# An encoder step with an expert layer: block loops written out, the end of a block taken apart

## The reference, cut to what matters

```python
def block(xb):                                   # PEER, xb: 128 normed tokens
    qh = (xb @ wq).reshape(PEER_BLOCK, PEER_HEADS, 2, PEER_HALF)
    s1 = jnp.einsum('thd,nd->thn', qh[:, :, 0], keys1)
    s2 = jnp.einsum('thd,nd->thn', qh[:, :, 1], keys2)
    v1, i1 = lax.top_k(s1, PEER_TOPK)
    v2, i2 = lax.top_k(s2, PEER_TOPK)
    ...                                          # 16 x 16 sums, top 16 of them: sc, e
    gate = jax.nn.softmax(sc, axis=-1)
    act = jax.nn.gelu(jnp.einsum('td,thkd->thk', xb, u_tab[e])) * gate
    return jnp.einsum('thk,thkd->td', act, v_tab[e])
...
hp = hp + yp                                     # yp: the mixer
hp = hp + peer(rmsnorm(hp, norm_ffn[l]), *pw)
...
y_prompt = rmsnorm(hp[:, N_META:], norm_final)
```

## Time and profile before

| what | value |
|---|---|
| median of 3 runs | 3307.91 us (3298.36 to 3314.12) |
| the profiled execution's own time | 3304.53 us |
| its span, first to last instruction | 3302.3 us |
| TensorE matmul busy | 2607.0 us (79%) |
| VectorE busy | 2282.9 us (69%) |
| GpSimd busy | 2004.0 us (61%) |
| ScalarE busy | 648.6 us (20%) |
| mean granted TensorE clock | 0.852 |
| DMA moved | 1213.81 MB, mean 368 GB/s |

### The profile page before, as it was taken

One profiled execution on the slowest core, in us unless ns is written; L12 is line 12 of the kernel. 1 busy time (PEld: TensorE's weight loads), 2 busy tenths in 40 slices (PEclk: granted clock), 3 DMA queues, 4 the chain that ended last, 5 costly groups with the idle time before them and its releaser, 6 DMA issues.

```text
span 3302.3 us, 42154 instructions
## 1 busy us (share of the span) xinstructions
PE 2607.0 (79%) x11764; PEld 1183.6 (36%) x11764; DVE 2282.9 (69%) x6088; ACT 648.6 (20%) x2367; POOL 2004.0 (61%) x2131
## 2 busy tenths in 40 slices
PE   7687888778887788778887788778887788777666
PEld 2563453234422453234422453234422453233111
DVE  2454987678756887679756887578766887679453
ACT  2221222111211222111211122112211222111111
POOL 0132567665776567665766567665776567665775
PEclk9798999878997889878987899878997889888557
DMA  7354999999999999999999999999999999999998
GB/s 263 135 197 166 387 363 394 416 390 344 396 405 403 377 368 395 409 391 349 399 402 398 376 368 398 407 392 343 404 413 400 371 368 399 403 398 359 398 399 362
DMA packets 340171, 1213.81 MB, mean 368 GB/s; under 512 B 41072, under 2 KB 41200, under 8 KB 339904
## 3 DMA queue, kind: packets, MB, share of 16 engines
q0 software_dynamic: 304128, 1107.43, 85.8%
q1 hardware_dynamic: 35776, 103.32, 8.3%
HBM read 1205.73 MB, written 4.87 MB: 367 GB/s over the span
## 4 chain that ended last, share of the span: by engine, by line
PE 25%; DMA 25%; DVE 24%; issue 15%; POOL 6%; ACT 3%; POOLq 0%; DVEq 0%; ACTq 0%; SPq 0%
DMA ring<-peer_v,idxv 16%; PE bank L458 15%; PE acc L458 10%; DMA ring<-peer_u,idx 9%; DVE ring L1434 8%; POOL ring L434 6%; DVE kw L1211 2%; DVE eh L1222 1%; DVE kw L1221 1%; DVE topi L1213 1%; DVE kw L1219 1%; ACT xn L857 1%; DVE idxv L1269 1%; DVE tops L1212 1%; DVE topi L1214 1%
## 5 line engine op out<-in xcount | busy, mean ns | idle before, releaser
L458 PE MATMUL acc<-ring,wv 128*32 128x512 f32 x4224 | 1312.9, 709 | 540.4 <-DMA ring<-peer_v,idxv 417.7
L1434 DVE SCALAR_TENSOR_TENSOR ring<-ring,xcur 128x1024 f32<-128x1024 f32 x1056 | 1283.6, 1218 | 656.4 <-DMA ring<-peer_u,idx 630.6
L434 POOL DMA_INDIRECT ring<-peer_u,idx x1056 | 1006.6, 953 | 817.7 <-issue 416.3
L434 POOL DMA_INDIRECT ring<-peer_v,idxv x1024 | 964.0, 941 | 433.5 <-issue 277.1
L458 PEld LDWEIGHTS acc<-ring,wv 128*32 128x32 f32 x4224 | 171.3, 115 | 1203.2 <-issue 662.7
L458 PEld LDWEIGHTS bank<-xT,win 128*128 128x128 f32 (+1 forms) x2304 | 276.2, 190 | 108.5 <-issue 92.9
L458 PE MATMUL bank<-xT,win 128*128 128x128 f32 (+1 forms) x2304 | 307.1, 290 | 6.8 <-DVE kw L1232 4.3
L857 ACT ACTIVATE wv<-rep,coefv 128x32 f32<-128x32 f32 x1024 | 264.3, 312 | 109.4 <-PE acc L458 79.4
L458 PEld LDWEIGHTS bank<-xT,qk 128*128 128x128 f32 x1024 | 160.1, 246 | 64.5 <-issue 64.5
L458 PE MATMUL bank<-win,xT 128*128 128x512 f32 (+3 forms) x368 | 177.3, 614 | 1.9 <-ACT xT L857 1.9
L458 PE MATMUL bank<-xT,qk 128*128 128x128 f32 x1024 | 173.1, 338 | 0.0
(11 more groups left out here) (232 smaller groups left out, 2213.8 us busy)
## 6 DMA issues: line engine op xcount, KB each, us to landing
qk<-wq SPq DMA_DIRECT2D x64, 512.0 KB
t<-wq SPq DMA_DIRECT2D x64, 512.0 KB, 6.9
ring<-peer_u,idx POOLq DMA_INDIRECT x1056, 6.5
ring<-peer_v,idxv POOLq DMA_INDIRECT x1024, 6.6
win<-w_in SPq DMA_DIRECT2D x6, 2048.0 KB, 15.3
ring<-wq SPq DMA_DIRECT2D x16, 512.0 KB, 5.2
wout<-w_out SPq DMA_DIRECT2D x1, 4096.0 KB, 22.4
xn<-x_prompt SPq DMA_DIRECT2D x8, 512.0 KB, 6.9
```

Source lines behind the costliest of these rows:

```text
L434: pool.indirect_dma_start(out=ring[:, slot, :], out_offset=None, in_=(peer_u, peer_v)[which], in_offset=bass.IndirectOffsetOnAxis(ap=rows_ ...
L458: return nc.tensor.matmul(out, lhsT, rhs, start=start, stop=stop)
L1434: stt(row, row, 1.0, xcur[:, :], ALU.mult, ALU.mult, accum_out=dots[:, column(b, e):column(b, e) + 1]).then_inc(s_dot, 1)
```

## The change

The five loops over blocks become Python loops, so that the code of every block stands in the program. What `is_count` and `looped` ask of a block's number is answered for each. At a block's end:

- TensorE's `take_up` is left to the sample alone. The first four V sums of a block open the banks of `acc` themselves (`start=opens`), the first of them after a wait for `s_acc_out`. The residual is added in ticks 22 to 25 by the new `add_residual`, one group of 32 tokens a tick, two matmuls of the shape of a V sum.
- ScalarE's `finish` is parted: `take_sums` (the copies out of `acc`) runs in tick 18 of the next block after that tick's `weights`, and raises `s_acc_out` at its end. `square_sums` runs in tick 19: squares of two halves into `xc`, an addition, Ln and Exp.
- VectorE's `finish` (the last norm, and with it `s_y`) runs at the beginning of tick 21.
- VectorE's waits in `query` for `s_acc0` and for V sums of the block before are taken out.
- SyncE's order stays as it is.

```diff
@@ constants
+T_RESIDUAL = LAG + GROUPS
@@ looped
-            return not isinstance(v, int)
+            return v > 2
@@ SyncE, GpSimd, TensorE, ScalarE, VectorE: the same edit in each
-            with sp.Fori(0, BLOCKS - 1) as b:
+            for b in range(BLOCKS - 1):
                 load_wq(b, range(10, 12))
                 load_x(b + 1, x_prompt[bass.ds(b * P + P, P), :])
                 load_wq(b, range(12, 16))
...
@@ TensorE: take_up keeps the sample's part alone
-                if b is None:
-                    pe.wait_ge(s_topk, 2)
-                else:
-                    pe.wait_ge(s_acc_out, streams_before(b))
-                if b is None:
-                    for half in range(2):
-                        last = mm(acc[0:n, 512 * half:512 * half + 512], ident[0:n, 0:n], h[0:n, 512 * half:512 * half + 512], stop=False)
-                else:
-                    mm(acc[:, 0:512], ident[:, :], h[:, 0:512], stop=False)
-                    for to, of in ((0, 64), (64, 0)):
-                        last = mm(acc[to:to + 64, 512:1024], ident[:, of:of + 64], h[:, 512:1024], stop=False)
+                pe.wait_ge(s_topk, 2)
+                for half in range(2):
+                    last = mm(acc[0:n, 512 * half:512 * half + 512], ident[0:n, 0:n], h[0:n, 512 * half:512 * half + 512], stop=False)
                 last.then_inc(s_acc0, 1)
+
+            def add_residual(b, tick):
+
+                g = tick - T_RESIDUAL
+                if not 0 <= g < GROUPS:
+                    return
+                if g == 0:
+                    pe.wait_ge(s_h2, streams_before(b) + 1)
+                for half in range(2):
+                    lo = SAMPLE * ((g + GROUPS // 2 * half) % GROUPS)
+                    last = mm(acc[lo:lo + SAMPLE, 512 * half:512 * half + 512], ident[:, SAMPLE * g:SAMPLE * g + SAMPLE],
+                              h[:, 512 * half:512 * half + 512], start=False, stop=False)
+                if g == GROUPS - 1:
+                    last.then_inc(s_acc0, 1)
@@ TensorE: expert_sum
+                opens = b is not None and j < GROUPS
+                if b is not None and j == 0:
+                    pe.wait_ge(s_acc_out, streams_before(b))
...
-                              ring[:, slot, 512 * half:512 * half + 512], start=False, stop=final)
+                              ring[:, slot, 512 * half:512 * half + 512], start=opens, stop=final)
@@ TensorE: the blocks
-            take_up(0)
-            with pe.Fori(0, BLOCKS - 1) as b:
+            for b in range(BLOCKS - 1):
                 for tick in range(LAG, BLOCK_TICKS):
                     expert_sum(b, tick - LAG)
+                    add_residual(b, tick)
                     beside(b, tick, True)
...
-                take_up(b + 1)
@@ ScalarE: finish is parted
-            def finish(b):
+            def take_sums(b):
...
-                    link(a(y, acc[0:n, :], ACT.Copy))
+                    last = a(y, acc[0:n, :], ACT.Copy)
                 else:
                     a(y[:, 0:512], acc[:, 0:512], ACT.Copy)
                     for to, of in ((0, 64), (64, 0)):
                         last = a(y[to:to + 64, 512:1024], acc[of:of + 64, 512:1024], ACT.Copy)
-                    link(last)
-                link(a(acc[0:n, :], y, ACT.Square, accum_out=stat[0:n, 6:7]))
-                act.sem_inc(s_acc_out, 1)
+                last.then_inc(s_acc_out, 1)
+
+            def square_sums(b):
+
+                n = n_experts(b)
+                y = xn[0:n, :]
+                junk = xc[:, :, :].rearrange("p f t -> p (f t)")[0:n, :]
+                act.wait_ge(s_acc_out, streams_before(b) + 1)
+                link(a(junk, y[:, 0:512], ACT.Square, accum_out=stat[0:n, 8:9]))
+                link(a(junk, y[:, 512:1024], ACT.Square, accum_out=stat[0:n, 7:8]))
+                link(a(stat[0:n, 6:7], stat[0:n, 7:8], ACT.Identity, bias=stat[0:n, 8:9]))
                 rstd(n, 6, D_MODEL).then_inc(s_rstd_y, 1)
+
+            def finish(b, tick):
+
+                done = b - 1 if b else None
+                if tick == LAG:
+                    restart()
+                    take_sums(done)
+                if tick == LAG + 1:
+                    square_sums(done)
@@ ScalarE: the blocks (after the last block take_sums and square_sums follow each other)
-            finish(None)
...
                     weights(b, tick - LAG)
+                    finish(b, tick)
                     beside(b, tick, True)
@@ VectorE: query
-                    if tick >= LAG and head > 0:
-                        dve.wait_ge(s_acc0, streams_before(b) + 1)
-                    elif not is_count(b, 0):
-                        dve.wait_ge(s_vsum, experts_before(b - 1) + TOPK * head + TOPK)
+                    if head >= PEER_HEADS - SAMPLE // TOPK:
+                        dve.wait_ge(s_vsum, SAMPLE)
@@ VectorE: the blocks
-            finish(None)
-            with dve.Fori(0, BLOCKS - 1) as b:
+            for b in range(BLOCKS - 1):
                 restart()
                 for tick in range(LAG, BLOCK_TICKS):
+                    if tick == LAG + 3:
+                        finish(b - 1 if b else None)
...
-                finish(b)

```

More of the change, by code:

```diff
@@ L448, in _ @@
             gathers(first + over(0), None)
-            with pool.Fori(0, BLOCKS - 1) as b:
+            for b in range(BLOCKS - 1):
                 gathers(side_by_side(b, range(LAG, P)) + over(b + 1), over(b)[-RING:])
@@ L1126, in _ @@
                 beside(0, tick, False)
-            finish(None)
-            with act.Fori(0, BLOCKS - 1) as b:
-                restart()
+            for b in range(BLOCKS - 1):
                 for tick in range(LAG, BLOCK_TICKS):
@@ L1158, in _ @@
                     spread_coef(b, PEER_HEADS - 1, tick)
-            finish(b)
+            take_sums(b)
+            square_sums(b)
         @block.vector
@@ L1530, in _ @@
             for tick in range(LAG, BLOCK_TICKS):
+                if tick == LAG + 3:
+                    finish(b - 1)
                 if tick % TOPK == 0:
```

## The result

The changed kernel takes 3346.78 us (median of 4 runs, 3340.25 to 3350.46); the kernel before, beside it on the same chip, 3311.01 us. The ratio is 1.0113, 95% interval 1.008 to 1.0146: slower. The profiled execution of the changed kernel took 3345.1 us against 3304.5 before, 40.6 us more, where the prediction's sum had 26.0. In the code after, the dot is L1458, `gmax` L1264, `tops` L1236, `idxv` L1293, the norm L1489; TensorE's helper is L459, SyncE's tile load L323, its store L336.

What follows compares the result with a forecast made beforehand. VectorE's path across each block's end was taken as the bound. Ends -43.6, norm +10.3, tile wait +46.1, spread +12.2, rest +1.0 sum to +26.0 us on the profiled 3304.53 us; forecast 3333 us, range 3290 to 3358.

Steps and rivals of the forecast that it cites:

- The gain at the ends: VectorE, last choice of a block to the next dot: the gap shrinks to 0.1 us, 43.6 us gained in all.
- The norm: VectorE, tick 21: the moved norm still costs 1.29 us an end, 10.3 us for eight.
- ticks 18 to 20 keep their shape: Ticks after the end: 9.3 us from the first dot to that of tick 21, as before.
- SyncE's queue: Tiles 10 and 11 stand behind the store awaiting the later norm; VectorE waits 5.8 us an end, 46.1 us for eight.
- The size of the wait: VectorE before head 5's choice, tick 25: 0.96 + 5.9 + 12.5 - 13.6 = 5.8 us an end, 46.1 us for eight.
- because GpSimd is being held back: Tile 10's landing taken as 5.9 us, between 5.2 and 6.9, with GpSimd held by VectorE, then TensorE.
- The chain: TensorE from tile 10's projection to head 5's second score: 12.5 us, first projection at the lower clock.
- The spread behind it: TensorE's V sum, residual and spread before VectorE's `idxv` copy, tick 25: 1.5 us an end, 12.2 us for eight.
- The signs: TensorE idle 7 to 9 us before tick 21's projection; VectorE 4 to 8 before `tops`, 1 to 2 before `idxv`.
- The small wait: Rival: landing and TensorE's work near their low ends, waits cancel the gain, time within 0.5% (3291 to 3324 us); 28%.
- The hidden wait: Rival: TensorE is ready within VectorE's four ticks, both waits go, -32 us, about 3275 us; 15%.
- Instruction supply: Rival: written-out code makes an engine stop for instructions; once a block on VectorE would be +22 us, slower; 5%.

Runs made afterwards that it cites:

- loops alone: The kernel before with its five loops over blocks written out and nothing moved; 3291.81 us, ratio 0.9931.
- ScalarE's store: The changed kernel with the stores of y inside the loop issued by ScalarE in tick 22 instead of SyncE; 3274.95 us, ratio 0.99.
- tiles first: The changed kernel with SyncE's order altered: tiles 10 and 11 loaded before the store of y; 3276.45 us, ratio 0.9895.
- gathers held back: The changed kernel with GpSimd issuing no gather from U row 24 of a block on until tile 10 has landed; 3327.9 us, ratio 1.0045.
- tile before the store: The changed kernel with tile 10 issued just ahead of the store of y, both still behind the norm; 3328.84 us, ratio 1.0045.
- norm a tick earlier: The changed kernel with VectorE's last norm in tick 20 instead of tick 21; 3304.46 us, ratio 0.9973.
- residual later: The changed kernel with the residual's matmuls in ticks 26 to 29 instead of 22 to 25; 3321.52 us, ratio 1.0026.
- tile 11 first: The changed kernel with tile 11 loaded before the store of y and tile 10 still behind it; 3358.01 us, ratio 1.0138.

## Why the prediction was right

*The gain at the ends* was 44.7 us (43.6 predicted), from the gap between `gmax` and the dot. The Trainium skill (Advanced Engine Details and Errata, section Control Flow Timing) gives a compare-and-branch about 108 ns, by an estimate 0.8 us for seven edges; a whole edge cost more, as the run with the loops alone shows, 2.4 us each on VectorE. What the branch alone takes no run here shows.

*The norm* came at 14.7 us for 10.3. Its 1.3 us are right; most of the missing 0.5 us an end is VectorE's wait for TensorE in tick 20 (6.3 us for eight ends, 2.8 before), which "ticks 18 to 20 keep their shape" passed over.

*SyncE's queue* was named rightly as what decides, with its place, its waiter and its releaser: two runs that free the tiles from the store, in two ways, take back 70 and 72 us. The Trainium skill (Perfetto Trace Analysis, section DMA Optimizations) advises, above all where there are loops or control flow, to consider separate issuing engines for inputs and outputs; the run with ScalarE's store agrees (3346.8 to 3275.0 us), and the run with the order altered shows that one queue does as well if nothing late stands ahead of an early need.

*The size of the wait* is the term that was off: 64.8 us measured, 46.1 predicted. For the end shown, the prediction's formula reads 0.5 (issue) + 8.3 (tile issued to projection) + 12.7 (TensorE's chain) - 13.6 = 7.9 us, against 0.96 + 5.9 + 12.5 - 13.6 = 5.8. VectorE's four ticks were right (13.62 us). The landing was not: 6.20 to 9.24 us, mean 8.05, seven of eight above the upper bound of 6.9. The step that failed was the choice of 5.9 "because GpSimd is being held back": at the end shown GpSimd issues three gathers in the 4.3 us ahead of the load and three more behind it. VectorE holds it for 2.38 and 1.02 us in between, and TensorE only from 1514.6 on. Before the change the end itself held the gathers back, to one or two in the 6 us ahead of the load; the change took that away along with the wait. The bounds were no bounds either: 5.2 and 6.9 are medians of other tiles, and the prologue's sixteen landed after 3.1 to 23.1 us.

The chain came out near its forecast, 12.7 us at the end shown and 12.9 in the mean, but its parts did not. The row of 3.26 us for a projection at the lower level holds 15 of its 16 matmuls, because the view ended at 3000 us; the whole took 3.48 us, at a granted clock of 0.56. Fully at the lower level the first projection took 3.75 us, and the sum behind it 1.68 instead of 1.05, where the forecast had the projection alone slowed. Against these 1.1 us stand overlaps of neighbours of 0.9 us in all, where the sum has 0.1. That agreement is luck.

That the total stayed under the upper bound of 3357 is luck in part too. The landing passed its bound by 1.15 us and the norm cost 0.5 us an end more, but the chain stayed 1.5 us under its bound of 14.4 us, because one sum ran slow, not two, and because of the overlaps; and the load was issued 0.54 us after the norm instead of 0.96.

*The spread behind it* cost 9.2 us for 12.2.

*The signs.* TensorE's idle time before the projection was 8.3 to 11.1 us (7 to 9 predicted), VectorE's before `tops` 5.5 to 9.0 (4 to 8), before `idxv` 1.1 to 1.5 (1 to 2), and a looped block took 376 us (374): the right waits with the right releasers, the first two larger than forecast.

*Rivals.* The small wait would have needed landings near 5.2 us; the shortest of the eight took 6.20. The hidden wait (about 3275 us) is the time of the kernel without the queue's fault, 3275 to 3276 us measured; it did not come about because no tile landed in 2 us. Instruction supply: VectorE's 15.5 us of waits on "issue" before its dots, six times in the kernel before, are absent after, and no such wait over 0.25 us came up inside the blocks on VectorE, ScalarE or TensorE's matmuls.

## What to carry to other kernels

When an event is moved later, list what stands behind its waiter in that queue, and when each of these is wanted: here 1.3 us of norm, moved three ticks, held two tiles that were wanted at once. Price a late load by landings beside the traffic that will be there, not by the mean: removing an idle stretch also removes the quiet in which its transfers used to land. And look for the cheap mend first: the same change with an input queue that holds no late output was 1% faster than before instead of 1.1% slower.

## What the runs showed of the hardware

A 512 KB tile's landing depended on what was issued just ahead of it. Gathers are counted in the 6 us ahead of the load, and from the load's issue to its landing.

| kernel | gathers ahead | gathers behind | store | landing, mean us |
|---|---|---|---|---|
| before | 1 to 2 | 1 to 3 | ahead | 4.90 |
| loops alone | 0 to 2 | 2 to 3 | ahead | 4.75 |
| gathers held back | 1 to 2 | 0 | ahead | 4.82 |
| tiles first; ScalarE's store | 2 to 4 | 2 to 4 | not near | 4.78; 5.11 |
| tile before the store | 3 to 4 | 3 | just behind | 6.61 |
| norm a tick earlier | 3 to 4 | 2 to 5 | ahead | 7.17 |
| after; residual later; tile 11 first | 3 | 3 | ahead | 8.05; 8.17; 8.56 |

The store alone does not lengthen the landing (first three rows); with three or four gathers ahead of it as well, it is longer by 2.3 to 3.7 us. That the gathers alone do not lengthen it is less sure: in the fourth row the tile is issued some 15 us earlier in the block, so its other traffic is not quite the same. How the chip shares its DMA engines among these transfers was not looked into.
